# Feed-forward of a decoder layer: the partial sum u4 ahead of the gate's products, p1c ahead of a tap, splits at the entrance shared out differently

## The chip, the cores and the metric

One Trainium2 chip, one of its cores. The metric is the device time of one execution in microseconds (us), lower is better. The engines are TensorE (PE in the profile), VectorE (DVE), ScalarE (ACT), GpSimd (POOL) and SyncE (SP, which here only issues DMA transfers). Each works through its own queue in order; they are tied together by semaphores, and every wait is written out in the kernel.

## The reference

One layer of a decoder on 1024 tokens of width 1024: gated mixing of attention and retention, cross-attention to a memory, and a feed-forward with a causal convolution. The change touches the feed-forward alone:

```python
up = causal_dwconv(rms_norm(h, g_ffn) @ w_up, w_conv, b_conv)   # 1024 -> 5632, three taps along the tokens
a, b = up[..., :D_FF], up[..., D_FF:]                           # D_FF = 2816
h = h + (silu(a) * b) @ w_down
return rms_norm(h, g_final)
```

Everything is float32. The row norm's factor is applied behind the product with `w_up`, and `g_ffn` ahead of it.

## The kernel before

**Splits.** PE multiplies float32 numbers in a rounded form, so each operand is split in two: a rounded high part (ACT copies it: `v_hi` for weights, `parts` for activations) and the rest, the low part (a subtraction: `v_lo` on POOL for weights, `lows` on DVE and a few lines on POOL for activations). Each product of two blocks is three matmuls, high by high, high by low, low by high (`product`, L1265, L1267, L1270).

**Rounds.** The feed-forward's way up runs in 22 rounds, numbered 0 to 21. Round i computes 128 columns of a and the matching 128 of b for all 1024 tokens. It treats these two column blocks and the two halves of the tokens as a 2 x 2 block product and does it in the manner of Strassen and Winograd: seven products instead of eight, each over four blocks of 128 along the inner dimension, so 7 x 4 x 3 = 84 matmuls of 128 x 512 a round. The sums on the activation side (t1 to t4, b2) are made once at the entrance, those on the weight side lie in memory from an earlier stage.

In a steady round PE's order (`seven`) is VA11, VS2, VS1, VS3, VA12, VS4, VA22; rounds 0 and 1 differ a little. The last three add to banks of PSUM that hold an earlier product, and an element-wise engine must have read that first:

- p1c: ACT copies the first product (VA11) from PSUM into the tile u4 (`p1_copy`).
- u2 = p1c + VS2, on DVE (`u_two`, L2721). PE waits for it ahead of VA12.
- u4 = u2 - VS1, on DVE (`u_four`, L2727). PE waits for it ahead of VS4, whose moving operand is b2h.
- c22 = u4 + VS3 (`quarters`, L2777), into zB. PE waits for it ahead of VA22.
- za0, c12 and c21 (L2785, L2789, L2750) bring the other quarters to zA and zB. POOL multiplies three of the four by the norm's factor (`scaled_by`, L624: zb0, zb1, za1).

**Convolution and gate.** A quarter then gets its three taps: ACT the first, with the bias (`tap`, L1942), DVE two more (`conv`, L2117; a1a and a1b for the upper half of a, b0a and b0b for the lower half of b, and so on). ACT applies silu (L1947), and DVE multiplies (`gates_mul`, L2766 and L2768: g0 and g1). ACT issues the store of the gated block yb (`gated_out`, L1952). The convolution and the gate of round i - 1 are done while PE is in round i.

**The order on each queue in a steady round** is written out by hand. DVE: c21, a1a, a1b, b0a, b0b, u2, b1a, b1b, g0, g1, u4, c22, za0, a0a, a0b, c12. ACT: tapA1, tapB1, the copy of VA22's weights, tapB0, silu, p1c, the copies of the next round's VA11, VS2 and VS1, the store of yb (which waits for g1), the copies of VS3 and VA12, tapA0, the copy of VS4, silu. POOL: zb0, the low parts of VA22, and of the next round's VA11, VS2, VS1 and VS3, then zb1, the low parts of VA12 and VS4, za1. The tuples `STEPS`, `TAPS` and `SCALES` name these positions; `v_at`, `a_at` and `p_at` turn a name into the count of the semaphore f_v (DVE), f_a (ACT) or f_p (POOL) at which that step is done. PE waits on these counts. SP loads the next weights as soon as the low part of the slot's last ones is made (`operand_loads`).

**The entrance.** The stage before is a product (`w_xo`) over eight blocks m of 128 channels. While it ends, DVE adds the residual (into hF), ACT squares it for the norm and makes the high part f0h, and DVE makes the low part f0l. From m = 4 on, ACT (`scaled`) and DVE (`mixed`) make the sums t1 to t4 and b2. ACT splits the first weights between blocks: VA11 and VS2 at m = 5, the rest at m = 6. POOL makes the low parts of these, of t3 (L630) and of t4 (L637). Three of the products of round 0 wait for such parts block by block. Between them PE sums the squares with 16 small matmuls, and turns the norm's factors with 8 transposing ones (L1149), which ACT copies to rbF; only then does ACT come to the weights of round 1.

After round 21 comes the way down (`step`), whose first operands are made in the last rounds.

Of the kernel before, what the change touches and what calls it, by code (L numbers as in the profile page):

```python
# [27 lines left out]
H2 = 512  # L28
# [75 lines left out]
STEPS = ("c21", "a1a", "a1b", "b0a", "b0b", "u2", "b1a", "b1b", "g0", "g1", "u4", "c22", "za0", "a0a", "a0b", "c12")  # L104
TAPS = ("tapA1", "tapB1", "tapB0", "silA1", "p1c", "tapA0", "silA0")
# [90 lines left out]
def build(nc, x, mem, pos, slabs, small, const, out):  # L196
# [23 lines left out]
    with ctx:  # L220
# [348 lines left out]
        def _(pool):  # L569
# [63 lines left out]
            pool.wait_ge(S["xT_lo"], lo_at("t1", 3))  # L633
            pool.wait_ge(S["f_p"], CH)
            for k in range(CH):
                pool.wait_ge(S["xT_hi"], hi_at("t4", k))
                pool.tensor_tensor(t4l[:, k, :], hF[:, CH + k, 0:H2], t4h[:, k, :].bitcast(f32), ALU.subtract).then_inc(  # L637
                    S["f_p"], 1)
# [748 lines left out]
        def _(act):  # L1387
# [489 lines left out]
            def p1_copy(i, e):  # L1877

                act.wait_ge(S["p_done"], done_at(i, VA11))
                if not (isinstance(i, int) and i == 0):  # L1880
                    act.wait_ge(S["f_v"], v_at(i - 1, "c22"))
                copy(u4[:, :], ps[:, 4 * e, :]).then_inc(S["f_a"], a_at(0, "p1c") if isinstance(i, int) and i == 0 else 1)
# [25 lines left out]
            for m in range(KB):  # L1908
                for b in range(2):
                    if m == KB - 1 and b == 1:  # L1910
                        act.wait_ge(d_done[1], USE0["xo"] + KB)
                        parts(0, 3)
                    square(1, m, b, USE0["xo"], hF, sq, f0h, "g_ffn")
                act.dma_start(s_y[m], hF[:, m, :]).then_inc(S["h_sp"], 16)
                if m + 2 < KB:
                    act.dma_start(hs[:, m % 2, :], s_h[m + 2]).then_inc(S[f"sa_ld{m % 2}"], 16)
                if m == KB - 1:
                    p1_copy(0, 0)
                if m >= CH:
                    scaled(m - CH)  # L1920
                if m == 5:
                    v_hi(0, VA11)
                    v_hi(0, VS2)
                if m == 6:
                    for v in (VS1, VS3, VA12, VS4):
                        v_hi(0, v)
# [13 lines left out]
            def tap(i, name, c, x_, b, z, y):  # L1940
                apart(act, i)
                act.activation(y[:, half(b)], z[:, 2 + b * H2:2 + (b + 1) * H2], ACT.Identity,  # L1942
                               scale=smc("cw2", c + FB * x_), bias=smc("b_conv", c + FB * x_)).then_inc(
                    S["f_a"], 1)
# [11 lines left out]
            def round_of(i, e, extra=()):  # L1956
# [4 lines left out]
                if not first:  # L1961
# [8 lines left out]
                    if last:  # L1970
                        extra[0]()
                    act.wait_ge(S["f_p"], p_at(i, "zb0"))
                    tap(i, "tapB0", p, 1, 0, zB, yb)
# [4 lines left out]
                    p1_copy(i, e)  # L1978
# [132 lines left out]
        def _(dve):  # L2111
# [612 lines left out]
            def u_four(i, e):  # L2724
# [3 lines left out]
                    S["f_v"], v_at(0, "u4") - v_at(0, "u2") if isinstance(i, int) and i == 0 else 1)  # L2728
# [25 lines left out]
            def gates_of(i):  # L2754
                gates_conv(i)
                gates_mul(i)
# [5 lines left out]
            def gates_mul(i):  # L2762
# [3 lines left out]
                dve.tensor_tensor(yb[:, half(0)], yb[:, half(0)], ya[:, half(0)], ALU.mult).then_inc(S["f_v"], 1)  # L2766
# [75 lines left out]
            dve.wait_ge(S["xT_lo"], lo_at("t1", 3))  # L2842
            dve.memset(zB[:, 0:2], 0.0).then_inc(S["cst"], 1)
            dve.wait_ge(S["cst"], 6)
            quarters(0, 0)
            with dve.Fori(0, (FB - 2) // 2) as i:
                for e in (1, 0):
# [3 lines left out]
                    gates_of(n)  # L2851
                    u_four(n, e)
# [4 lines left out]
            gates_of(n)  # L2857
            u_four(n, 1)
# [8 lines left out]
            gates_mul(FB)  # L2867
# [150 lines left out]
```

## Time and profile before

| | |
|---|---|
| three timed runs | 1844.48, 1847.39, 1847.49 us; median 1847.39 us |
| the profiled execution, its own time | 1844.24 us |
| its span from first to last instruction | 1842.4 us |
| instructions | 25311 |
| PE busy | 1783.6 us (97%) |
| DVE busy | 1076.6 us (58%) |
| ACT busy | 698.7 us (38%) |
| POOL busy | 986.4 us (54%) |
| granted clock of TensorE, mean | 0.99 of full |
| feed-forward, way up | about 1171 to 1616 us of the span |

The profile is one execution. "Busy" of PE counts matmuls that overlap in the pipeline, so 97% doesn't say how closely they follow each other; that is seen in the start times. A row of the order of time gives the start, the duration, the engine, the line of the kernel, the operation and its tiles (output <- inputs), and in brackets how long the engine had been idle ahead of it and which instruction ended that. Lines L1389 (a copy on ACT), L2114 (a low part on DVE) and L2117 (a multiply-add on DVE) are helpers that many steps share, so these are told apart by their tiles. The tiles u2 and u4 both show as u.

### The profile page before, as it was taken

The page shows a single profiled execution, that of the slowest core. Times are in us where ns is not written, and L with a number is a line of the kernel's source. Part 1 is how long each engine was busy: PE and PEld are TensorE (multiplying, and loading weights), DVE is VectorE, ACT ScalarE, POOL GpSimd, SP SyncE. Part 2 cuts the span into 40 slices and gives each one's busy share as a digit, 9 for nine tenths or more (in the row PEclk, how much of TensorE's full clock was granted, in tenths as well). Part 3 has the DMA queues.
Part 4 walks back from the last instruction along what each step waited for, and adds up shares of the span by engine and source line. Part 5 has one row for each costly group of instructions (what it writes and reads, how often), then busy time and mean ns, then how long its engine had stood idle before and what let it go on. Part 6 is the DMA issues. An engine that isn't in the chain of part 4 may idle for free.

```text
span 1842.4 us, 25311 instructions
## 1 busy us (share of the span) xinstructions
PE 1783.6 (97%) x8724; PEld 1481.4 (80%) x8724; DVE 1076.6 (58%) x1549; ACT 698.7 (38%) x1249; POOL 986.4 (54%) x559
## 2 busy tenths in 40 slices
PE   6999999999999899999999989989999999999998
PEld 6788888888887777778878878778888888888887
DVE  5355445101342877885345553877777877789852
ACT  7422223211012666731133222544444444454432
POOL 6833333446664577644532223477777777665540
PEclk9999999999999999999999999899999999999999
DMA  6511111346671688673221224234333333485322
GB/s 261 205 46 35 34 34 46 126 178 210 244 246 45 219 304 322 219 274 128 101 80 47 68 81 138 91 103 135 110 125 126 113 132 119 159 310 175 121 81 92
DMA packets 111054, 261.83 MB, mean 142 GB/s; under 512 B 7680, under 2 KB 50304, under 8 KB 106496
## 3 DMA queue, kind: packets, MB, share of 16 engines
q1 hardware_dynamic: 84720, 182.13, 29.6%
q10 hardware_dynamic: 26256, 78.65, 11.4%
q8 instruction: 50, 0.82, 0.2%
q14 instruction: 28, 0.23, 0.0%
HBM read 186.82 MB, written 73.92 MB: 142 GB/s over the span
## 4 chain that ended last, share of the span: by engine, by line
PE 83%; DVE 7%; ACT 4%; POOL 3%; issue 2%; DMA 1%; SPq 0%; DVEq 0%; ACTq 0%; POOLq 0%
PE ps L690 15%; PE ps L695 15%; PE ps L696 15%; PE ps L1265 7%; PE ps L1270 7%; PE ps L1267 7%; PE ps L1341 3%; PE ps L1340 3%; PE ps L1342 3%; POOL wl L576 1%; ACT prow L1703 1%; PE ps L1069 1%; DVE aneg L2460 1%; DMA raw<-in_slabs 1%; PE ps L1049 1%
## 5 line engine op out<-in xcount | busy, mean ns | idle before, releaser
L583 POOL TENSOR_SCALAR wh<-raw 128x1024 fp32r<-128x1024 f32 x76 | 212.7, 2799 | 496.7 <-PE ps L690 488.0
L690 PE MATMUL ps<-uh,wh 128*128 128x512 f32 (+1 forms) x576 | 228.4, 397 | 2.4 <-POOL wl L585 2.4
L696 PE MATMUL ps<-uh,wl 128*128 128x512 f32 (+1 forms) x576 | 225.2, 391 | 0.0
L695 PE MATMUL ps<-ul,wh 128*128 128x512 f32 (+1 forms) x576 | 224.9, 390 | 0.0
L585 POOL TENSOR_TENSOR wl<-raw,wh 128x1024 fp32r<-128x1024 f32 x76 | 183.5, 2415 | 6.3
L617 POOL TENSOR_TENSOR wl<-raw,wh 128x512 fp32r<-128x512 f32 x88 | 140.9, 1621 | 34.3 <-ACT wh L1389 34.3
L604 POOL TENSOR_TENSOR over_rings<-over_rings 128x512 f32<-128x512 f32 x92 | 118.1, 1285 | 51.7 <-DMA over_rings<-in_slabs 46.1
L2117 DVE SCALAR_TENSOR_TENSOR ya<-zA,sm,ya 128x512 f32<-128x512 f32 x88 | 90.9, 1033 | 81.1 <-ACT ya L1942 73.9
L2117 DVE SCALAR_TENSOR_TENSOR yb<-zB,sm,yb 128x512 f32<-128x512 f32 x88 | 126.6, 1438 | 13.4 <-ACT yb L1942 7.2
L665 POOL TENSOR_TENSOR wl<-raw,wh 128x512 fp32r<-128x512 f32 x63 | 93.9, 1499 | 72.6 <-ACT wh L1389 72.6
L690 PEld LDWEIGHTS ps<-uh,wh 128*128 128x128 f32 (+1 forms) x576 | 107.2, 186 | 25.1 <-POOL wl L585 2.6
L696 PEld LDWEIGHTS ps<-uh,wl 128*128 128x128 f32 (+1 forms) x576 | 107.0, 186 | 25.0 <-issue 0.8
L695 PEld LDWEIGHTS ps<-ul,wh 128*128 128x128 f32 (+1 forms) x576 | 107.2, 186 | 22.9 <-issue 0.5
L1389 ACT ACTIVATE wh<-raw 128x512 fp32r<-128x512 f32 (+1 forms) x163 | 104.1, 653 | 41.4 <-DMA raw<-in_slabs 20.3
L617 POOL TENSOR_TENSOR wl<-ssm,wh 128x512 fp32r<-128x512 f32 x44 | 67.2, 1530 | 74.3 <-ACT wh L1389 74.3
L1342 PE MATMUL ps<-mvh_,wl 128*128 128x512 f32 x252 | 98.0, 389 | 0.0
L1340 PE MATMUL ps<-mvh_,wh 128*128 128x512 f32 x252 | 98.0, 389 | 0.0
L1341 PE MATMUL ps<-mvl_,wh 128*128 128x512 f32 x252 | 98.0, 389 | 0.0
L2356 DVE TENSOR_TENSOR mxr<-ps,sig 128x512 f32<-128x512 f32 x16 | 11.1, 692 | 148.0 <-PE ps L696 148.0
L1265 PE MATMUL ps<-f0h,wh 128*128 128x512 f32 x176 | 69.4, 394 | 5.7 <-DVE u L2721 3.0
L1389 ACT ACTIVATE wh<-ssm 128x512 fp32r<-128x512 f32 x44 | 27.6, 631 | 123.4 <-PE ps L1270 66.2
L1267 PE MATMUL ps<-f0l,wh 128*128 128x512 f32 x176 | 69.1, 393 | 0.0
(461 smaller groups left out, 4914.9 us busy)
## 6 DMA issues: line engine op xcount, KB each, us to landing
raw<-in_slabs SPq DMA_DIRECT2D x110, 512.0 KB, 3.5
over_rings<-in_slabs SPq DMA_DIRECT2D x22, 1024.0 KB, 7.2
s_s<-over_rings SPq DMA_DIRECT2D x22, 1024.0 KB, 4.8
ssm<-s_s SPq DMA_DIRECT2D x22, 512.0 KB, 3.7
raw<-s_s SPq DMA_DIRECT2D x22, 512.0 KB, 4.7
s_f<-yb ACTq DMA_DIRECT2D x22, 512.0 KB, 2.6
raw<-s_d SPq DMA_DIRECT2D x36, 256.0 KB, 2.5
dsum<-in_slabs SPq DMA_DIRECT2D x16, 512.0 KB, 7.1
```

The lines of the kernel that those rows point to most:

```text
L583: pool.tensor_scalar(wh[:, j, :], raw[:, j % RAWS, :], 1.0, None, ALU.mult).then_inc(S["w_hi"], 1)
L585: pool.tensor_tensor(wl[:, j, :], raw[:, j % RAWS, :], wh[:, j, :].bitcast(f32), ALU.subtract).then_inc(S["w_ready"], 1)
L617: pool.tensor_tensor(wl[:, v // 2, half(v % 2)], src, wh[:, v // 2, half(v % 2)].bitcast(f32), ALU.subtract).then_inc(S["v_ready"], 1)
L690: l = pe.matmul(o, lh, rh, start=start, stop=False)
L695: pe.matmul(o, lh, rl, start=False, stop=False)
L696: return pe.matmul(o, ll, rh, start=False, stop=stop)
L1265: l = pe.matmul(ps[:, bank, :], wh_, xh[:, k0 + k, :], start=not more and k == 0, stop=False, skip_group_check=True)
L1267: l = pe.matmul(ps[:, bank, :], wh_, xl[:, k0 + k, :], start=False, stop=False, skip_group_check=True)
L1340: pe.matmul(o, wh[:, j, cm], fh_, start=p == 0 and q < 5, stop=False, skip_group_check=True)
L1341: pe.matmul(o, wh[:, j, cm], fl_, start=False, stop=False, skip_group_check=True)
L1342: l = pe.matmul(o, wl[:, j, cm], fh_, start=False, stop=p == NP - 1, skip_group_check=True)
L2117: return dve.scalar_tensor_tensor(out=o, in0=a, scalar=s_, in1=b_, op0=op0, op1=op1)
```

## The change

1. DVE's order: u4 moves from behind g0 and g1 to between b1b and g0 (`gates_of` now calls `u_four` between `gates_conv` and `gates_mul`). The names in `STEPS` move along, and the counts of the rounds outside the loop are mended to fit.
2. ACT's order: p1c moves from behind tapB0 and the silu to ahead of tapB0, with `TAPS` to match.
3. At the entrance ACT copies VS1 and VS3 of round 0 at m = 5 instead of m = 6.
4. The four low parts of t4 move from POOL to DVE, behind the low parts of b2 and ahead of `quarters(0, 0)`.

```diff
--- before.py
+++ after.py
@@ -101,8 +101,8 @@
 
 VA11, VS2, VS1, VS3, VA12, VS4, VA22 = range(7)
 NV = 7
-STEPS = ("c21", "a1a", "a1b", "b0a", "b0b", "u2", "b1a", "b1b", "g0", "g1", "u4", "c22", "za0", "a0a", "a0b", "c12")
-TAPS = ("tapA1", "tapB1", "tapB0", "silA1", "p1c", "tapA0", "silA0")
+STEPS = ("c21", "a1a", "a1b", "b0a", "b0b", "u2", "b1a", "b1b", "u4", "g0", "g1", "c22", "za0", "a0a", "a0b", "c12")
+TAPS = ("tapA1", "tapB1", "p1c", "tapB0", "silA1", "tapA0", "silA0")
 SCALES = ("zb0", "zb1", "za1")
 
 
@@ -630,12 +630,6 @@
                 pool.tensor_tensor(t3l[:, k, :], hF[:, k, H2:T], t3h[:, k, :].bitcast(f32), ALU.subtract).then_inc(
                     S["f_p"], 1)
             v_lo(0, VA22)
-            pool.wait_ge(S["xT_lo"], lo_at("t1", 3))
-            pool.wait_ge(S["f_p"], CH)
-            for k in range(CH):
-                pool.wait_ge(S["xT_hi"], hi_at("t4", k))
-                pool.tensor_tensor(t4l[:, k, :], hF[:, CH + k, 0:H2], t4h[:, k, :].bitcast(f32), ALU.subtract).then_inc(
-                    S["f_p"], 1)
 
             def round_of(i, extra=None):
 
@@ -1879,7 +1873,7 @@
                 act.wait_ge(S["p_done"], done_at(i, VA11))
                 if not (isinstance(i, int) and i == 0):
                     act.wait_ge(S["f_v"], v_at(i - 1, "c22"))
-                copy(u4[:, :], ps[:, 4 * e, :]).then_inc(S["f_a"], a_at(0, "p1c") if isinstance(i, int) and i == 0 else 1)
+                copy(u4[:, :], ps[:, 4 * e, :]).then_inc(S["f_a"], a_at(0, "tapA0") - 1 if isinstance(i, int) and i == 0 else 1)
 
 
             def scaled(k):
@@ -1919,10 +1913,10 @@
                 if m >= CH:
                     scaled(m - CH)
                 if m == 5:
-                    v_hi(0, VA11)
-                    v_hi(0, VS2)
+                    for v in (VA11, VS2, VS1, VS3):
+                        v_hi(0, v)
                 if m == 6:
-                    for v in (VS1, VS3, VA12, VS4):
+                    for v in (VA12, VS4):
                         v_hi(0, v)
             parts(3, 7)
             acc_hi(1, acc, ach)
@@ -1937,11 +1931,11 @@
             rms_copy(1, rbF)
 
 
-            def tap(i, name, c, x_, b, z, y):
+            def tap(i, name, c, x_, b, z, y, steps=1):
                 apart(act, i)
                 act.activation(y[:, half(b)], z[:, 2 + b * H2:2 + (b + 1) * H2], ACT.Identity,
                                scale=smc("cw2", c + FB * x_), bias=smc("b_conv", c + FB * x_)).then_inc(
-                    S["f_a"], 1)
+                    S["f_a"], steps)
 
             def silu(b):
                 act.activation(ya[:, half(b)], ya[:, half(b)], ACT.Silu).then_inc(S["f_a"], 1)
@@ -1969,13 +1963,14 @@
                         v_hi(i, VA22)
                     if last:
                         extra[0]()
+                    else:
+                        p1_copy(i, e)
                     act.wait_ge(S["f_p"], p_at(i, "zb0"))
-                    tap(i, "tapB0", p, 1, 0, zB, yb)
+                    tap(i, "tapB0", p, 1, 0, zB, yb, 2 if last else 1)
                     act.wait_ge(S["f_v"], v_at(i, "a1b"))
                     silu(1)
                     if last:
                         return
-                    p1_copy(i, e)
                 if extra:
                     extra[0]()
                 else:
@@ -2725,7 +2720,7 @@
                 dve.wait_ge(S["p_done"], done_at(i, VS1))
                 own(i, "u2")
                 dve.tensor_tensor(u4[:, :], u2[:, :], ps[:, 4 * e + 2, :], ALU.subtract).then_inc(
-                    S["f_v"], v_at(0, "u4") - v_at(0, "u2") if isinstance(i, int) and i == 0 else 1)
+                    S["f_v"], v_at(0, "c22") - 1 - v_at(0, "u2") if isinstance(i, int) and i == 0 else 1)
 
             def z_of(z, b):
                 return z[:, 2 + b * H2:2 + (b + 1) * H2]
@@ -2751,19 +2746,20 @@
                 conv(i, p, 0, 1, zA, ya, "tapA1", ("a1a", "a1b"))
                 conv(i, p, 1, 0, zB, yb, "tapB0", ("b0a", "b0b"))
 
-            def gates_of(i):
+            def gates_of(i, e):
                 gates_conv(i)
+                u_four(i, e)
                 gates_mul(i)
 
             def gates_conv(i, steps=1):
                 p = i - 1
                 conv(i, p, 1, 1, zB, yb, "tapB1", ("b1a", "b1b"), steps)
 
-            def gates_mul(i):
+            def gates_mul(i, steps=1):
                 p = i - 1
                 dve.wait_ge(S["f_a"], a_at(p, "silA0"))
                 own(i, "b1b")
-                dve.tensor_tensor(yb[:, half(0)], yb[:, half(0)], ya[:, half(0)], ALU.mult).then_inc(S["f_v"], 1)
+                dve.tensor_tensor(yb[:, half(0)], yb[:, half(0)], ya[:, half(0)], ALU.mult).then_inc(S["f_v"], steps)
                 dve.wait_ge(S["f_a"], a_at(i, "silA1"))
                 dve.tensor_tensor(yb[:, half(1)], yb[:, half(1)], ya[:, half(1)], ALU.mult).then_inc(S["f_v"], 1)
 
@@ -2840,6 +2836,9 @@
             lows(2 * CH, 3 * CH)
             dve.wait_ge(S["f_p"], CH)
             dve.wait_ge(S["xT_lo"], lo_at("t1", 3))
+            for k in range(CH):
+                dve.wait_ge(S["xT_hi"], hi_at("t4", k))
+                lo(t4l[:, k, :], hF[:, CH + k, 0:H2], t4h[:, k, :]).then_inc(S["f_p"], 1)
             dve.memset(zB[:, 0:2], 0.0).then_inc(S["cst"], 1)
             dve.wait_ge(S["cst"], 6)
             quarters(0, 0)
@@ -2848,14 +2847,12 @@
                     n = 2 * i + (2 - e)
                     rest_of(n, e)
                     u_two(n, e)
-                    gates_of(n)
-                    u_four(n, e)
+                    gates_of(n, e)
                     quarters(n, e)
             n = FB - 1
             rest_of(n, 1)
             u_two(n, 1)
-            gates_of(n)
-            u_four(n, 1)
+            gates_of(n, 1)
             move_lo(0)
             quarters(n, 1, (lambda: move_lo(1),))
             move_lo(2)
@@ -2864,7 +2861,7 @@
             move_lo(4)
             gates_conv(FB, 2)
             move_lo(5)
-            gates_mul(FB)
+            gates_mul(FB, 2)
             for n in range(6, NSTEP):
                 move_lo(n)
                 if 0 <= n - 9 < NP:
```

## Rows read from the trace of the kernel before

**Rows 1.** Stretches: length, busy us (x instructions) by engine, PEclk, DMA share, GB/s
```profile
1166.00:1199.00 33.00, 29.26 (x118) 22.77 (x116) 30.95 (x30) 22.41 (x40) 20.77 (x14) 0.84 0.24 80
1262.00:1455.00 193.00, 192.50 (x840) 156.67 (x840) 149.40 (x160) 87.16 (x140) 141.71 (x101) 1.00 0.37 122
```

**Rows 2.** Order of time, PE, rounds 1, 3, 20: start, duration, instruction, [idle]
```profile
1217.04 0.50 PE L1265 MATMUL ps<-f0h,wh 128*128 128x512 f32 x1 [3.00 <-DVE u L2721]
...
1221.75 0.50 PE L1265 MATMUL ps<-b2h,wh 128*128 128x512 f32 x1 [1.69 <-DVE u L2727]
...
1257.53 0.39 PE L1265 MATMUL ps<-f0h,wh 128*128 128x512 f32 x1
...
1260.03 0.39 PE L1270 MATMUL ps<-f0h,wl 128*128 128x512 f32 x1
...
1589.01 0.49 PE L1265 MATMUL ps<-b2h,wh 128*128 128x512 f32 x1
```

**Rows 3.** Order of time, DVE, from round 12 to round 13
```profile
1448.89 2.88 DVE L2117 SCALAR_TENSOR_TENSOR yb<-zB,sm,yb 128x512 f32<-128x512 f32 x2
1451.80 0.69 DVE L2766 TENSOR_TENSOR yb<-yb,ya 128x512 f32<-128x512 f32 x1
1452.41 0.69 DVE L2768 TENSOR_TENSOR yb<-yb,ya 128x512 f32<-128x512 f32 x1
1453.01 0.68 DVE L2727 TENSOR_TENSOR u<-u,ps 128x512 f32<-128x512 f32 x1
...
1464.35 1.30 DVE L2117 SCALAR_TENSOR_TENSOR yb<-zB,sm,yb 128x512 f32<-128x512 f32 x1 [0.41 <-ACT yb L1942]
...
1471.64 0.69 DVE L2768 TENSOR_TENSOR yb<-yb,ya 128x512 f32<-128x512 f32 x1
```

**Rows 4.** Order of time, ACT (ACTq is its queue of DMA issues), same rounds
```profile
1453.30 0.34 ACTq L1952 DMA_DIRECT2D s_f<-yb  x1
1453.77 0.63 ACT L1389 ACTIVATE wh<-ssm 128x512 fp32r<-128x512 f32 x1 [4.82 <-PE ps L1270]
...
1461.40 0.82 ACT L1942 ACTIVATE ya<-zA,sm 128x512 f32<-128x512 f32 x1 [1.66 <-POOL zA L624]
...
1463.35 0.80 ACT L1942 ACTIVATE yb<-zB,sm 128x512 f32<-128x512 f32 x1
...
1464.58 0.58 ACT L1389 ACTIVATE u<-ps 128x512 f32<-128x512 f32 x1
```

**Rows 5.** Order of time, POOL, same rounds
```profile
1454.48 1.30 POOL L617 TENSOR_TENSOR wl<-ssm,wh 128x512 fp32r<-128x512 f32 x1 [3.26 <-ACT wh L1389]
...
1460.20 1.08 POOL L624 TENSOR_TENSOR zA<-zA,rbF 128x512 f32<-128x512 f32 x1
...
1463.52 1.57 POOL L617 TENSOR_TENSOR wl<-a,wh 128x512 fp32r<-128x512 f32 x1 [1.19 <-ACT wh L1389]
```

**Rows 6.** Order of time, POOL, the entrance and round 1
```profile
1170.68 3.43 POOL L617 TENSOR_TENSOR wl<-raw,wh 128x512 fp32r<-128x512 f32 x2
...
1192.47 6.36 POOL L637 TENSOR_TENSOR t4l<-hF,t4h 128x512 fp32r<-128x512 f32 x4
1198.78 3.00 POOL L617 TENSOR_TENSOR wl<-raw,wh 128x512 fp32r<-128x512 f32 x2
...
1208.78 1.09 POOL L624 TENSOR_TENSOR zA<-zA,rbF 128x512 f32<-128x512 f32 x1
```

**Rows 7.** Order of time, DVE, the entrance
```profile
1171.18 1.77 DVE L2117 SCALAR_TENSOR_TENSOR hF<-hF,sm,tx 128x512 f32<-128x512 f32 x1
1172.88 1.78 DVE L2117 SCALAR_TENSOR_TENSOR f0l<-hF,sm,f0h 128x512 fp32r<-128x512 f32 x1
...
1192.55 5.12 DVE L2114 TENSOR_TENSOR b2l<-hF,b2h 128x512 fp32r<-128x512 f32 x3
```

**Rows 8.** Order of time, PE, the entrance
```profile
1177.06 0.50 PE L1265 MATMUL ps<-f0h,wh 128*128 128x512 f32 x1 [2.73 <-ACT u L1389]
...
1195.89 1.03 PE L1149 MATMUL ps<-cn,rsm 128*128 128x128 f32 x8
```

## The prediction

> **What bounds the kernel now.** I read the page first: TensorE is busy nearly everywhere, so a part counts only where PE waits or where something sets PE's pace. The diff touches the feed-forward alone. The stretch table [rows 1] splits it in two: an entrance (1166 to 1199 us) with a granted clock of 0.84, and rounds at clock 1.00 in which PE took 193.00 us for 840 matmuls. A round is 7 products of 12 matmuls, so that is ten rounds of 19.3 us.
>
> PE's order of time [rows 2] says what a round could take: inside a product the starts are (1260.03 - 1257.53) / 11 = 0.227 us apart, 84 x 0.227 = 19.07 us. The first matmul of VS4 (the one on b2h) is at 1221.75 in round 1 and at 1589.01 in round 20: 367.26 / 19 = 19.33 us. So PE loses 0.26 us a round, 4.9 us in 19 rounds, and in PE's order of time the gap lies at that same matmul in each of them, the one that waits for u4. In round 1 it waits 1.69 us for u4 and, a product earlier, 3.00 us for u2 [rows 2].
>
> Why is u4 late by the same small amount every round? I followed it backwards through DVE, ACT and POOL. g1 (L2768) starts at 1452.41 and ends at 1453.10 [rows 3]; ACT issues the store of yb at 1453.30 and then, because its queue is in order, copies wh for VS3 at 1453.77 (the row names PE, but the product it means is long over; it is the store ahead that holds the queue) [rows 4]. POOL had been idle 3.26 us until that copy was done; it starts at 1454.48 and its za1 product ends at 1460.20 + 1.08 = 1461.28 [rows 5]. ACT's tapA1 starts at 1461.40, behind an idle 1.66 us that POOL ended [rows 4]. Then come the two taps on ya, the b0 pair, u2, the b1 pair, g0 and the next g1, at 1471.64 [rows 3]. That is a **closed loop of DVE, ACT and POOL, from g1 to g1**, without PE in it: 19.23 us here and 19.33 in the mean, as PE's own rounds show. PE needs 19.07 and follows the loop. What lengthens g1 to g1 lengthens every round; what only brings u4 forward does not.
>
> **Part 1: u4 ahead of g0 and g1.** u4 is 0.60 us of DVE (1452.41 to 1453.01 is one start to the next) and now lies before g1, in the loop. It gives a little back: g0 reads what b1b wrote and starts only at 1451.80, the pair having ended at 1448.89 + 2.88 = 1451.77, while independent neighbours start 0.09 us before the end of the one ahead (1453.01 against 1453.10) [rows 3]. u4 doesn't read b1b's result and fills that hold of 0.11. g1 comes 0.49 us later, and with it the store, the copy of VS3, POOL's queue (VS3, zb1, VA12, VS4, za1) and tapA1. Nothing absorbs it that I can find: POOL was idle before that copy, not after it. From round 1 to round 20 there are 19 passes: 19 x 0.49 = **+9.3 us**. Bounds: 0.30 a pass (5.7), if a DVE operation that now falls elsewhere beside POOL saves some of it; 0.60 (11.4), without the filled hold. In exchange u4 itself starts 1453.01 - 1451.80 + 0.11 = 1.3 us earlier against its round. That is a gain **once**, -1.3 us, since the loop sets the pace. It is needed in full, as in round 1 PE waited 1.69 us for u4. The last round, 21, is half unrolled with other work in it; PE didn't wait there before, so I count no pass for it.
>
> **Part 2: the copy of the first product (p1c) ahead of tapB0.** ACT's copy lasts 0.58 us (the row at 1464.58) and tapB0 starts that much later than 1463.35 [rows 4]. b0a is next in the loop: it was ready at 1464.35, having waited 0.41 us for tapB0. Yet it took 1.30 us, and ended at 1465.65, 0.56 us after POOL's split of VA22 (1463.52 + 1.57 = 1465.09) [rows 3, 5]. So b0a stood behind POOL's operation. Ready at 1464.93 it would still stand there, and end when it did. Price 0, cover 0.16 us thick. Without the cover it is 0.48 to 0.58 a pass, 19 x 0.5 = 9.5 us; a gain isn't excluded either, since u2 can no longer wait for p1c, but it didn't wait before. The Trainium skill (SBUF — State Buffer, Who interferes with whom) says that a VectorE instruction with two SBUF inputs and a GpSimd instruction that reads SBUF exclude each other for the whole instruction; by that rule the trace agrees (1.30 us for b0a against 0.69 for g1, beside which POOL was idle).
>
> **Part 3: two splits (VS1, VS3) at m = 5 of the entrance instead of m = 6.** ACT and POOL are idle then. POOL did VA12 and VS4 at 1170.68 to 1174.11 [rows 6], behind VS1 and VS3; with those done a block earlier it ends about 3.0 us earlier, at 1171.1. DVE's last f0l at 1172.88 took 1.78 us beside it [rows 7], as did the operation ahead; both (1.77 and 1.78) fall to about 0.7. I take 2.1 off DVE's chain, less 0.25 for what the moved pair costs it at its new place (around 1160, ahead of a wait for PE): 1.85. PE's second product waited 2.73 us (ACT's copy at the end of that chain) [rows 8] and starts 1.85 earlier. Splits and partial sums hang on the same chain, so the entrance shifts by that.
>
> **Part 4: the four t4l from POOL to DVE.** POOL spent 6.36 us on them from 1192.47, and round 1's splits followed at 1198.78 without a pause [rows 6]. These end at the za1 product of 1208.78, which tapA1, b0 and u2 of round 1 stand behind, PE's wait of 3.00. Off POOL, what is late next? ACT's copies for round 1 come behind rbF, and that behind PE's small matmuls at 1195.89 + 1.03 [rows 8], after VS3. These can move only with PE: 1.85 us by part 3, and more if PE keeps its clock (the 0.84 cost it 33 x 0.16 = 5.3 us in the entrance [rows 1], of which I give at most 2.3 to this place). Before, POOL began 1198.78 - 1196.92 = 1.9 us after them; now that is at 1196.9, or down to 1194.6: 1.9 to 4.2 us off round 1. On DVE the four cost 0.6 each beside an idle POOL (g1's 0.60 from start to start [rows 3]), 2.4 us, but b2l ahead of them took 5.12 for three beside POOL [rows 7] and falls to about 1.8. c22 of round 0 then comes near 1196, before VS4 is done: hidden; if DVE stays slow, 4 x 1.7 = 6.8 us, and up to 2 us of it on PE's path. Nothing else changes queue; SP's loads for round 1 stand behind the a22 load and shift with the chain. Parts 3 and 4 together: **-2.4 us**, nearer the slow end, since the waits among which the low clock stood mostly stay. Ends: -4.5 and -1.0.
>
> **Sum.** +9.3 - 1.3 - 2.4 = **+5.6 us**. The profiled execution took 1844.24 us (span 1842.4 and 1.8 around it), so 1849.8; the median of the three timed runs is 3.15 higher. The four executions average 1845.9, and I predict 1851.5. Forecast alone: 5.7 - 1.3 - 4.5 = -0.1 to 11.4 - 1.3 - 1.0 = +9.1, so 1846 to 1855.
>
> **Rivals.**
> A. *PE's gaps are the whole of it* (the other side). u4's wait is the only one PE has in a steady round, and u4 comes 1.3 us earlier: all 4.9 us return, with 1.3 in round 1 and 2.4 at the entrance: -8.6, 1837.3 us. It needs g1 to have room of 0.49 us and the loop to be able to run at 19.07. Against it: POOL's 3.26 us of idleness ended by ACT directly behind the store [rows 5]. The Trainium skill (Perfetto Trace Analysis, Optimization Strategy) tells one to find the gaps of the most-contended engine and make what it waits for start sooner; by that advice the change is right and this rival's time follows. Chance 0.18.
> B. *The later g1 is absorbed but the loop keeps its pace*: rounds of 19.33 as before, and only the gains that come once: -1.3 - 2.4 = -3.7, 1842.2 us. It would need a hidden gap between g1 and tapA1. Chance 0.11.
> C. *The cover of part 2 is too thin*: POOL's split comes earlier or DVE gets the memory first, and tapB0's shift enters the loop: 19 x 0.49 more, 1860.8 us. It decides as soon as b0a is ready after POOL's VA22 split ends. Chance 0.09.
> Forecast 0.62.
>
> **How the numbers follow.** About 0.2% (3.7 us) is what a measurement of this kernel can tell from no change. Slower: five sixths of the forecast, 0.52, and C, 0.09: 0.61. Faster: A and nearly half of B, 0.22. Same: the rest, 0.17. The range goes from 1840, which takes in B and the edge of A, to 1858.
>
> **What the changed profile would show.** g1 start to g1 start 19.8 us; PE's gap ahead of VS4 0.7 to 0.8 us instead of 0.1 to 0.4, and nowhere else in a round; ACT's copy of VS3 0.49 us later after b1b; b0a still ending 0.56 us behind POOL's VA22 split; PE's wait after the first product about 0.9 us; POOL's first split of round 1 near 1197; round 1's VS4 about 3.7 us earlier than 1221.75, round 20's about 5.6 later than 1589.01. I'm wrong if rounds come at 19.1 (A), 19.3 (B) or 20.3 (C).

## The result and the profile after

| | before | after |
|---|---|---|
| timed runs, median (lowest to highest) | 1846.56 (1843.84 to 1847.49) us, 9 runs | 1850.15 (1849.29 to 1853.58) us, 9 runs |
| ratio after to before, 95% interval | | 1.0029 (1.002 to 1.0038) |
| the profiled execution, its own time | 1844.24 us | 1850.15 us |
| its span | 1842.4 us | 1848.3 us |
| DVE, ACT, POOL busy | 1076.6, 698.7, 986.4 us | 1069.2, 693.0, 976.5 us |

The kernel is slower by 0.3%, though three engines are busy for less time and PE's wait at the entrance has shrunk. The medians differ by 3.6 us, the means of the nine runs by 5.05, the spans of the two profiles by 5.9. The time went where the forecast put it, into the rounds; inside, three terms were off and happened to cancel.

The stretches of the changed kernel, in the columns of [rows 1]:

```profile
1166.00:1199.00 33.00, 31.15 (x132) 24.79 (x131) 28.70 (x37) 24.14 (x42) 13.94 (x10) 0.90 0.25 85
1262.00:1455.00 193.00, 189.25 (x821) 152.34 (x820) 142.94 (x158) 81.18 (x136) 139.38 (x98) 1.00 0.35 119
```

The same 193 us of rounds hold fewer instructions on every engine (821 matmuls for 840), while the entrance holds more of PE's (132 for 118) and POOL is busy there for 13.94 us in place of 20.77.

DVE's order of time in rounds 1, 3 and 20 (start, duration, instruction, idle ahead of it):

```profile
1217.67 0.68 DVE L2764 TENSOR_TENSOR yb<-yb,ya 128x512 f32<-128x512 f32 x1
...
1249.96 0.98 DVE L2112 SCALAR_TENSOR_TENSOR yb<-zB,sm,yb 128x512 f32<-128x512 f32 x1 [0.72 <-ACT yb L1936]
...
1253.26 2.88 DVE L2112 SCALAR_TENSOR_TENSOR yb<-zB,sm,yb 128x512 f32<-128x512 f32 x2
1256.06 0.67 DVE L2722 TENSOR_TENSOR u<-u,ps 128x512 f32<-128x512 f32 x1
1256.65 0.68 DVE L2762 TENSOR_TENSOR yb<-yb,ya 128x512 f32<-128x512 f32 x1
1257.26 0.68 DVE L2764 TENSOR_TENSOR yb<-yb,ya 128x512 f32<-128x512 f32 x1
...
1593.35 0.68 DVE L2764 TENSOR_TENSOR yb<-yb,ya 128x512 f32<-128x512 f32 x1
```

g1 starts at 1217.67 in round 1 and at 1593.35 in round 20: 375.68 / 19 = 19.77 us a round, where the kernel before had 19.33. u4 now starts 0.08 us before the b1 pair's end (1253.26 + 2.88 = 1256.14), in place of g0's hold.

What follows g1 on ACT and POOL in round 3, and POOL's split of VA22 half a round earlier:

```profile
1258.14 0.35 ACTq L1946 DMA_DIRECT2D s_f<-yb  x1
1258.62 0.64 ACT L1383 ACTIVATE wh<-ssm 128x512 fp32r<-128x512 f32 x1 [6.76 <-DVE zB L2773]
```

```profile
1248.66 1.75 POOL L617 TENSOR_TENSOR wl<-a,wh 128x512 fp32r<-128x512 f32 x1 [1.31 <-ACT wh L1383]
...
1259.33 1.30 POOL L617 TENSOR_TENSOR wl<-ssm,wh 128x512 fp32r<-128x512 f32 x1 [3.75 <-ACT wh L1383]
```

ACT's copy of VS3 starts 1258.62 - 1256.14 = 2.48 us after the b1 pair, against 1453.77 - 1451.77 = 2.00 before [rows 3, 4]; POOL's idleness ahead of VS3 is 3.75 us for 3.26 [rows 5]. b0a ends at 1250.94, 0.53 us behind POOL's VA22 (1250.41).

PE at the entrance (the second product, the third) and at VS4 in rounds 1, 4 and 20:

```profile
1175.75 0.50 PE L1259 MATMUL ps<-f0h,wh 128*128 128x512 f32 x1 [0.75 <-ACT u L1383]
...
1181.73 0.50 PE L1259 MATMUL ps<-t2h,wh 128*128 128x512 f32 x1 [0.93 <-DVE t2l L2109]
...
1218.29 0.39 PE L1259 MATMUL ps<-b2h,wh 128*128 128x512 f32 x1
...
1275.85 0.39 PE L1264 MATMUL ps<-f0h,wl 128*128 128x512 f32 x1
1276.59 0.49 PE L1259 MATMUL ps<-b2h,wh 128*128 128x512 f32 x1 [0.35 <-DVE u L2722]
...
1592.95 0.49 PE L1259 MATMUL ps<-b2h,wh 128*128 128x512 f32 x1 [0.39 <-DVE u L2722]
```

In round 4 the two starts at VS4 are 0.74 us apart, so 0.51 us are lost (0.45 to 0.56 in rounds 3 to 20), and a further 0.10 us at the next start, which the kernel before loses too. PE's list of waits from 1210 to 1700 us (what it waited for, us in total, times, longest):

```profile
PE ps L1259 <- DVE u L2722: 6.7, 18, 0.4
PE ps L1259 <- DVE u L2716: 2.8, 1, 2.8
PE ps L1334 <- DVE mvl_ L2109: 1.0, 1, 1.0
```

The third line is new, and belongs to the way down. DVE and PE there, first in the kernel before, then in the changed one:

```profile
1625.79 0.68 DVE L2114 TENSOR_TENSOR mvl_<-b,mvh_ 128x512 fp32r<-128x512 f32 x1
```

```profile
1627.24 0.39 PE L1340 MATMUL ps<-mvh_,wh 128*128 128x512 f32 x1
```

```profile
1631.70 0.68 DVE L2109 TENSOR_TENSOR mvl_<-b,mvh_ 128x512 fp32r<-128x512 f32 x1
```

```profile
1632.53 0.47 PE L1334 MATMUL ps<-mvh_,wh 128*128 128x512 f32 x1 [1.00 <-DVE mvl_ L2109]
```

**Where the 5.9 us of span went.** The program up to the feed-forward does not take the same time twice. DVE's first read of that stage's last block from PSUM comes here, before and after:

```profile
1166.28 0.69 DVE L2680 TENSOR_TENSOR hF<-ps,hs 128x512 f32<-128x512 f32 x1 [1.82 <-PE ps L696]
```

```profile
1166.95 0.69 DVE L2675 TENSOR_TENSOR hF<-ps,hs 128x512 f32<-128x512 f32 x1 [1.35 <-PE ps L690]
```

All that follows, the experiments too, is counted from that read ("the mark"), since single spans differ by more than some of the terms. Of the edits only part 3 reaches ahead of it (ACT and POOL do its splits some 8 us earlier), and there too DVE is still waiting for PE at the mark, 1.35 to 1.54 us. Changes against the kernel before:

| place | from the mark, before | after | change |
|---|---|---|---|
| g1 of round 1 | 54.13 | 50.72 | -3.41 (of it +0.49 for standing behind u4: the entrance itself gave -3.9) |
| g1 of round 20 | 421.32 | 426.40 | +5.08 |
| PE's VS4, round 20 | 422.73 | 426.00 | +3.27 |
| end of the span | 676.1 | 681.35 | +5.2 |

19 rounds cost 19 x 0.447 = +8.5. PE comes out of them 3.3 us late, DVE 5.1 us late, and the end of the span is as late as DVE was.

### The profile page after: what moved, and what is told of

Read it like the earlier page. It is cut to its first block, busy times and chain, and to the rows that moved or that the text cites. A ratio compares the mean times of both kernels' runs of the same rounds, so it can differ in the third digit from the quotient of the medians.

```text
span 1848.3 us, 25311 instructions
## 1 busy us (share of the span) xinstructions
PE 1785.5 (97%) x8724; PEld 1480.3 (80%) x8724; DVE 1069.2 (58%) x1553; ACT 693.0 (37%) x1249; POOL 976.5 (53%) x555
## 4 chain that ended last, share of the span: by engine, by line
PE 63%; POOL 13%; issue 12%; DVE 7%; ACT 3%; DMA 1%; POOLq 0%; SPq 0%; DVEq 0%; ACTq 0%
PE ps L684 15%; PE ps L689 15%; PE ps L690 15%; POOL wl L617 10%; PE ps L1334 3%; PE ps L1335 3%; PE ps L1336 3%; POOL zB L624 2%; PE ps L1063 1%; ACT prow L1697 1%; DVE aneg L2455 1%; PE ps L1043 1%; PE ps L1357 1%; PE ps L1359 1%; PE ps L1358 1%
## 5 line engine op out<-in xcount | busy, mean ns | idle before, releaser
L2112 DVE SCALAR_TENSOR_TENSOR ya<-zA,sm,ya 128x512 f32<-128x512 f32 x88 | 100.3, 1140 | 87.5 <-ACT ya L1936 80.4
L2112 DVE SCALAR_TENSOR_TENSOR yb<-zB,sm,yb 128x512 f32<-128x512 f32 x88 | 115.4, 1312 | 23.7 <-ACT yb L1936 17.5
```

Source lines behind the costliest of these rows:

```text
L2112: return dve.scalar_tensor_tensor(out=o, in0=a, scalar=s_, in1=b_, op0=op0, op1=op1)
```

## The experiments

The theory is the closed loop of the prediction, whose pace u4 has lengthened; its first rival is A, which takes PE's waits for the bound. Each kernel is one edit of the kernel before or of the changed one. "A round" is (g1 of round 20 - g1 of round 1) / 19 in its profile.

### Part 1 alone, and the change without it

`u4_only` is the kernel before with part 1; `no_u4` is the changed kernel with part 1 undone.

```diff
-STEPS = (..., "b1a", "b1b", "g0", "g1", "u4", "c22", ...)
+STEPS = (..., "b1a", "b1b", "u4", "g0", "g1", "c22", ...)
                 gates_conv(i)
+                u_four(i, e)
                 gates_mul(i)
...
-                    u_four(n, e)
```

> The kernel before with part 1 alone (u4 ahead of g0 and g1 on DVE). Theory (the closed loop of DVE, ACT and POOL from g1 to g1 sets the rounds, and u4 now lies in it): g1 to g1 goes from 19.33 to 19.77 us as in the changed kernel, 19 passes are +8.5 us at g1 of round 20; PE's VS4 of round 20 is only 7.2 us later, since u4 itself comes 1.3 us earlier in the round, but the way down waits for DVE and takes that back: +8.5 us in all. Rival (PE's waits for u4 are the whole of it; the loss came from p1c delaying tapB0): rounds of 19.07, 1.3 us less wait in round 1, about -6 us in all.

> The changed kernel with part 1 undone: p1c ahead of tapB0 and both edits at the entrance stay. Theory: rounds of 19.33 us as before (the p1c edit costs nothing, because b0a ends 0.55 us behind POOL's split of VA22 either way), the entrance keeps its 3.9 us: round 1's b1b about 3.9 us earlier than before, and so the end: -3.9 us, 7.5 to 8.5 us better than the changed kernel with all its parts. Rival (p1c ahead of tapB0 lengthens the loop): rounds of 19.6 to 19.8 us, +1 to +5 us against before.

Measured: `u4_only` 1853.79 us against 1845.47, ratio 1.0045 (1.003 to 1.0061), a round (1598.54 - 1222.31) / 19 = 19.80 us. `no_u4` 1839.58 us, ratio 0.9967 (0.9954 to 0.9981), a round (1582.49 - 1216.20) / 19 = 19.28. So part 1 costs 0.47 to 0.49 us a round (19.80 against 19.33, 19.77 against 19.28), 9.0 to 9.4 us in 19 rounds, with or without the rest; by the timed runs of `u4_only` it costs 8.3 us, and the other three parts gain 5.9. Rival A falls: with part 1 alone PE's list reads

```profile
PE ps L1265 <- DVE u L2727: 6.1, 17, 0.4
...
PE ps L1340 <- DVE mvl_ L2114: 1.0, 1, 1.0
```

The step that PE waits for was moved forward in its round, and PE waits for it 17 times in the list; in the kernel before the same list names u4 once, with 1.7 us.

**Part 2 gains a little.** It was not tried alone, but parts 3 and 4 leave the rounds at 19.32 and 19.33 us (`splits_only` and `t4l_only` below), so what else separates two kernels is part 2's: 19.28 for 19.33 without part 1, 19.77 for 19.80 with it. The rounds come in pairs, a shorter and a longer one: from g1 to g1 19.22 and 19.44 us in the kernel before, 19.22 and 19.34 in `no_u4`, 19.70 and 19.91 in `u4_only`, 19.72 and 19.83 in the changed kernel. Part 2 takes 0.1 us off the longer one and nothing off the shorter, which is the one that [rows 3] to [rows 5] show. The longer one of the kernel before, whose g1 started at 1471.64, on POOL and DVE:

```profile
1485.20 1.29 POOL L617 TENSOR_TENSOR wl<-raw,wh 128x512 fp32r<-128x512 f32 x1 [0.60 <-ACT wh L1389]
```

```profile
1485.35 1.69 DVE L2117 SCALAR_TENSOR_TENSOR yb<-zB,sm,yb 128x512 f32<-128x512 f32 x1 [0.20 <-DVE yb L2117]
```

and of `no_u4`, on POOL and DVE:

```profile
1480.24 1.30 POOL L617 TENSOR_TENSOR wl<-raw,wh 128x512 fp32r<-128x512 f32 x1 [0.48 <-ACT wh L1383]
```

```profile
1466.79 0.68 DVE L2763 TENSOR_TENSOR yb<-yb,ya 128x512 f32<-128x512 f32 x1
...
1480.50 1.58 DVE L2112 SCALAR_TENSOR_TENSOR yb<-zB,sm,yb 128x512 f32<-128x512 f32 x1 [0.20 <-DVE yb L2112]
```

From g1 POOL's split of VA11 starts after 13.56 us before and after 13.45 with part 2, because ACT's copies ahead of it come 0.11 us earlier. b0b ends 0.54 to 0.55 us behind that split in both, so it, u2 and the next g1 come 0.1 us earlier too.

### The store of yb behind the next two copies

If the loop goes g1, store, copy of VS3, POOL, then ACT's copies of VS3 and VA12 need not stand behind the store that waits for g1. `store_late` does that to the kernel before, `after_store_late` to the changed one.

```diff
-                if not first:
-                    gated_out(i)
                 if extra:
+                    if not first:
+                        gated_out(i)
                     extra[1]()
                 else:
                     v_hi(i + 1, VS3)
                     v_hi(i + 1, VA12)
+                    if not first:
+                        gated_out(i)
```

> The kernel before with one edit: on ACT the store of yb, which waits for g1, is issued behind the copies of VS3 and VA12 instead of ahead of them. Theory: this opens the loop at the place where ACT's in-order queue ties it; POOL's queue then waits for c22 (zb1) instead, about 1.3 us earlier, the loop falls below PE's 19.07 us, PE's waits for u4 vanish from round 3 or so on: rounds of 19.05 to 19.1 us, 19 x 0.26 = -4.9 us. Rival (the tie is not the store's place: DVE's load and its standing behind POOL set 19.33): rounds unchanged, within 1 us of before.

> The changed kernel with the same late store. Theory: rounds of 19.05 to 19.1 us here too, since u4 ahead of g1 costs nothing once g1 is on no loop; with the entrance's 3.9 us and the shorter wait of round 1 the sum is -3.9 - 1.3 - 4.9, near -9 us against before, and PE has no wait for u4 at all. If the order u4, g0, g1 costs by itself (c22 comes no earlier than before, and zb1 hangs on it), the gain over before is only some 4 us and rounds stay at 19.3 or more.

Measured: `store_late` 1866.69 us against 1845.47, ratio 1.0112 (1.0095 to 1.0128), a round (1608.94 - 1223.79) / 19 = 20.27: the opposite of what I expected. `after_store_late` 1836.91 us, ratio 0.9953 (0.9938 to 0.9967), a round (1580.88 - 1217.76) / 19 = 19.11: as expected, PE's own pace with hardly a wait. Of the first, PE's list says

```profile
PE ps L1265 <- DVE u L2729: 19.6, 20, 1.1
```

and in the orders of time of DVE, PE and POOL, one round of it:

```profile
1466.68 1.78 DVE L2770 TENSOR_TENSOR yb<-yb,ya 128x512 f32<-128x512 f32 x1
1468.38 0.67 DVE L2729 TENSOR_TENSOR u<-u,ps 128x512 f32<-128x512 f32 x1
...
1472.95 1.83 DVE L2119 SCALAR_TENSOR_TENSOR ya<-zA,sm,ya 128x512 f32<-128x512 f32 x1 [0.20 <-DVE ya L2119]
1474.70 0.67 DVE L2791 TENSOR_TENSOR zA<-u,ps 128x512 f32<-128x512 f32 x1
```

```profile
1469.18 0.49 PE L1265 MATMUL ps<-b2h,wh 128*128 128x512 f32 x1 [1.12 <-DVE u L2729]
```

```profile
1466.09 1.82 POOL L617 TENSOR_TENSOR wl<-ssm,wh 128x512 fp32r<-128x512 f32 x1 [0.60 <-ACT wh L1389]
...
1472.94 1.29 POOL L617 TENSOR_TENSOR wl<-raw,wh 128x512 fp32r<-128x512 f32 x1 [0.73 <-ACT wh L1389]
1475.45 1.09 POOL L624 TENSOR_TENSOR zA<-zA,rbF 128x512 f32<-128x512 f32 x1 [1.22 <-DVE zA L2791]
```

Brought forward, POOL's split of VS3 (1466.09 to 1467.91) falls onto g1, which takes 1.78 us instead of 0.68, and ends 0.55 us behind it. u4 stands behind g1, so it is 1.1 us later; PE waits 1.12 us for it and starts VS4 late; ACT's copy of the VS4 weights waits 0.80 us for PE; POOL's split of VS4 waits for ACT and now falls onto a0b (1.83 us; in the kernel before a0b took 1.50). c12 and with it POOL's za1, **idle for 1.22 us where the kernel before had none ahead of it**, come late, and so does tapA1. There is a second closed path, from u4 over c22, za0, tapA0, a0a, a0b and c12 to za1, with a branch from u4 through PE's VS4. My prediction had seen only the first.

In the changed kernel the same edit finds u4 ahead of g1. POOL's VS3 split then lengthens only g0, which u4 doesn't wait for; in `after_store_late`:

```profile
1465.09 1.18 DVE L2764 TENSOR_TENSOR yb<-yb,ya 128x512 f32<-128x512 f32 x1
```

### An extra operation of the same length, ahead of g1 or behind it

To weigh the two paths by themselves, DVE reads the bank of PSUM once more (0.68 us, 0.60 from start to start, the result is not used), in the changed order ahead of u4 and so of g1 (`extra_ahead`), or in the old order behind g1 and ahead of u4 (`extra_behind`).

```diff
                 own(i, "u2")
+                if not (isinstance(i, int) and i == 0):
+                    dve.tensor_reduce(amax[:, 0, 0:1], ps[:, 4 * e + 2, :], AX.X, ALU.max)
                 dve.tensor_tensor(u4[:, :], u2[:, :], ps[:, 4 * e + 2, :], ALU.subtract)
```

> The kernel before with part 1, and in each round from 1 on one more VectorE operation that nothing needs, a reduction of the same PSUM bank (128 x 512, about 0.6 us), ahead of u4 and so ahead of g0 and g1. Theory: it lies in the loop from g1 to g1 in full: rounds of 19.80 + 0.6 = 20.4 us, and 19 x 0.6 = 11 us more than part 1 alone, about +20 us against before. Rival (VectorE has room in a round, 19.3 of which it is busy for some 15): rounds as with part 1 alone, 19.8 us.

> The kernel before, with the same extra operation ahead of u4, but g0 and g1 stay ahead of both: it lies behind g1. Theory: g1 and the store aren't touched, so the loop keeps 19.33 us; u4 is 0.6 us later in the round, once. But u4 also leads through PE's VS4, ACT's copy of the next VS4 and POOL's split to za1, a path that was about 0.6 us shorter than the one by g1, so it may just begin to show: rounds of 19.3 to 19.5 us, 0 to +4 us. Rival (any work on VectorE before PE's operand costs its own length every round): 19.9 us, +12 us.

Measured, one execution each: `extra_ahead` 1869.74 us, a round (1609.16 - 1221.60) / 19 = 20.40, so +0.60 on the 19.80 of `u4_only`, as expected. In all it is 23.7 us above the kernel before, some 4 more than expected, and from the mark 3.9 of its 25.3 us come on the way down, where PE waits 2.1 us for a low part of POOL. `extra_behind` 1860.04 us, a round (1602.77 - 1220.17) / 19 = 20.14, so +0.81 on 19.33, where I expected up to 0.2 and the rival said 0.6. An operation behind g1 costs more than its own length. DVE's order of time in it, and POOL's:

```profile
1461.89 0.69 DVE L2770 TENSOR_TENSOR yb<-yb,ya 128x512 f32<-128x512 f32 x1
1462.49 0.68 DVE L2728 TENSOR_REDUCE amax<-ps 128x1 f32<-128x512 f32 x1
...
1466.34 1.76 DVE L2117 SCALAR_TENSOR_TENSOR ya<-zA,sm,ya 128x512 f32<-128x512 f32 x1 [1.24 <-ACT ya L1942]
...
1469.72 0.68 DVE L2791 TENSOR_TENSOR zA<-u,ps 128x512 f32<-128x512 f32 x1
```

```profile
1465.20 1.10 POOL L624 TENSOR_TENSOR zB<-zB,rbF 128x512 f32<-128x512 f32 x1
1466.25 3.00 POOL L617 TENSOR_TENSOR wl<-raw,wh 128x512 fp32r<-128x512 f32 x2
...
1470.48 1.09 POOL L624 TENSOR_TENSOR zA<-zA,rbF 128x512 f32<-128x512 f32 x1 [1.23 <-DVE zA L2791]
```

and the same place in the kernel before, on DVE and on POOL:

```profile
1456.26 1.12 DVE L2117 SCALAR_TENSOR_TENSOR ya<-zA,sm,ya 128x512 f32<-128x512 f32 x1 [1.24 <-ACT ya L1942]
...
1459.00 0.68 DVE L2789 TENSOR_TENSOR zA<-u,ps 128x512 f32<-128x512 f32 x1
```

```profile
1455.73 1.10 POOL L624 TENSOR_TENSOR zB<-zB,rbF 128x512 f32<-128x512 f32 x1
1456.78 3.45 POOL L617 TENSOR_TENSOR wl<-raw,wh 128x512 fp32r<-128x512 f32 x2
```

In each case a0a becomes ready while POOL is at work, and ends 0.55 us behind the operation that it finds there. Before, that is zb1, which ends at 1456.83: a0a ends at 1457.38, and it is POOL's split of VA12 (the first of the pair), begun in the meantime, that takes longer, 1.75 us. In `extra_behind` a0a is ready 0.09 us after that split has begun: the split takes 1.30 us and ends at 1467.55, and a0a takes 1.76 and ends at 1468.10. The 0.60 us of the extra operation have become 1.24 us at a0a's end. From g1 to za1 it is 1470.48 - 1461.89 = 8.59 us, against 1460.20 - 1452.41 = 7.79 before: +0.80, the whole +0.81. The rest of the 1.24 went into the room that the old order had there: za1 came 0.52 us after c12's end (1460.20 against 1459.68), and now comes 0.08 after it.

### The entrance: each part alone

`splits_only` is the kernel before with part 3, `t4l_only` with part 4.

```diff
                 if m == 5:
-                    v_hi(0, VA11)
-                    v_hi(0, VS2)
+                    for v in (VA11, VS2, VS1, VS3):
+                        v_hi(0, v)
```

```diff
-            for k in range(CH):
-                pool.wait_ge(S["xT_hi"], hi_at("t4", k))
-                pool.tensor_tensor(t4l[:, k, :], ...)
...
+            for k in range(CH):
+                dve.wait_ge(S["xT_hi"], hi_at("t4", k))
+                lo(t4l[:, k, :], hF[:, CH + k, 0:H2], t4h[:, k, :]).then_inc(S["f_p"], 1)
```

> The kernel before with part 3 alone (VS1 and VS3 split at m = 5). Theory: DVE's chain of the entrance comes 2.0 us earlier (POOL is out of its way at the last f0l), PE's wait behind the first product falls from 2.7 to 0.7 us; t4l stays on POOL and ends 2.0 us earlier, so round 1 and the end come 2.0 us earlier. Rounds 19.33. Rival (the entrance's gain is t4l's alone): 0.

> The kernel before with part 4 alone (the four low parts of t4 on DVE). Theory: POOL is free early, but ACT's copies for round 1 stand behind PE's small matmuls, which nothing moves: POOL starts round 1's splits at 1198.7 instead of 1198.8; with less in DVE's way round 1 comes 0.1 to 1 us earlier. The part pays only together with part 3, whose 2.0 us become 3.9 with it. Rival (POOL's 6.4 us were the bound by themselves): -2 us or more.

Measured: `splits_only` 1844.34 us against 1846.0, ratio 0.9993 (0.9984 to 1.0002); `t4l_only` 1843.91, ratio 0.9991 (0.9982 to 1.0). Both intervals reach 1, so the profiles decide, from the mark to g1 of round 1: `splits_only` 52.07, that is -2.06; `t4l_only` 53.37, -0.76; both together -3.8 (`no_u4`, 50.31). They give more together than the sum of 2.8, and POOL shows why. First `splits_only`, then `t4l_only`, then the changed kernel:

```profile
1194.91 6.82 POOL L637 TENSOR_TENSOR t4l<-hF,t4h 128x512 fp32r<-128x512 f32 x4
1201.70 2.53 POOL L617 TENSOR_TENSOR wl<-raw,wh 128x512 fp32r<-128x512 f32 x2
```

```profile
1200.61 2.55 POOL L617 TENSOR_TENSOR wl<-raw,wh 128x512 fp32r<-128x512 f32 x2 [6.07 <-ACT wh L1383]
```

```profile
1196.19 2.59 POOL L617 TENSOR_TENSOR wl<-raw,wh 128x512 fp32r<-128x512 f32 x2 [4.96 <-ACT wh L1383]
```

From the mark, round 1's first split starts at 32.50 before, 31.01 with part 3 alone (POOL is still at t4l), 32.29 with part 4 alone (POOL idles, waiting for ACT's copy behind rbF, behind PE), 29.24 with both. Each part takes away one of two bounds that lay close together.

### The first partial sum and the late store together, and the fastest version

`u4_store_late` is the kernel before with part 1 and the late store: two edits that cost 8.3 and 21.2 us by themselves. `all_za1_early` is the changed kernel with the late store, and in round 0 alone POOL's za1 stands directly behind zb1:

```diff
                 scaled_by(i, "zb1", zB, 1, v_at(i, "c22"), 2 if first else 1)
+                if first:
+                    scaled_by(i, "za1", zA, 1, v_at(i, "c12"))
                 for v in (VA12, VS4):
...
-                scaled_by(i, "za1", zA, 1, v_at(i, "c12"))
+                if not first:
+                    scaled_by(i, "za1", zA, 1, v_at(i, "c12"))
```

> The kernel before with two edits: u4 ahead of g0 and g1 (alone +8.3 us) and the store of yb behind the copies of VS3 and VA12 (alone +21 us). Theory: a round has two closed paths, one by g1, the store and POOL's queue, one by u4, c22, PE's VS4 and c12 to za1. Each edit alone shortens the one and lengthens the other; together g1 is on neither and u4 is 1.1 us (g0 and g1) earlier on the second. So rounds of 19.1 us, PE's own pace; round 1 waits 1.3 us less for u4: -1.3 - 19 x 0.23 = -5.7 us against before. Rival (the costs of the two edits add): +29 us.

> The changed kernel with the late store and, in round 0 alone, POOL's za1 product directly behind zb1, ahead of the splits of VA12 and VS4. With the late store PE waits only at the entrance, 2.74 us of it in round 1 for u2, which stands behind tapA1 and tapB0. Theory: za1 comes about 2.4 us earlier, but zb0 of round 1, which tapB0 needs, stays behind the two splits: u2 and the end 1.2 us earlier than with the late store alone, -9.8 us against before, ratio 0.9947. Rival (za1 wasn't what round 1 waited for): -8.6 us.

Measured, against 1845.35 us for the kernel before (14 runs; a fifteenth took 6317.33 us and is not counted): `u4_store_late` 1840.79 us, 4.6 less, ratio 0.9979 (0.9964 to 0.9993), a round (1581.06 - 1216.95) / 19 = 19.16; from the mark its span ends 3.2 us earlier. Both gains are below the 5.7 us expected: u4's wait of 1.7 us in round 1 is gone, but the one for u2 ahead of it is 4.1 us for 3.0. `all_za1_early` 1835.16 us, ratio 0.9949 (0.993 to 0.9968), a round (1580.02 - 1216.95) / 19 = 19.11; PE's wait for u2 in round 1 is 2.0 us for the 2.7 of `after_store_late`. It has the lowest median made here, 10.2 us below the kernel before. But the intervals of the two overlap, and from the mark their spans end within 0.2 us of each other, so that za1's new place gains anything is not shown.

That the two harmful edits gain together follows from the two paths. Part 1 shortens the path from u4 and lengthens the one from g1. The late store cuts the path from g1, but POOL's split now falls on the product that DVE does at that time: g1 in the old order, with u4 behind it, and g0 in the new one, which u4 doesn't wait for. The late store in turn makes g1's lateness harmless.

## Why the prediction was right, and which of its steps were not

The forecast of +5.6 us met +5.9 of span (+5.2 from the mark), and its 1851.5 us a median of 1850.15. Point by point:

- **Part 1, the closed loop and its pace: right.** Its 0.49 us a round measured 0.47 (`u4_only` against the kernel before) and 0.49 (the changed kernel against `no_u4`), so 9.0 to 9.4 us for the 9.3 written. Rounds of 19.8 were forecast, 19.77 measured. The gap ahead of VS4 is 0.5 us, smaller than the 0.7 to 0.8 written, since PE loses its 0.65 us a round (19.72 less 19.07) in two places, 0.55 there and 0.10 at the start behind it. The kernel before lost 0.06 and 0.27 us there by turns, and the same 0.10.
- **Part 2 at nothing: wrong by a little.** The cover held: b0a, ready later, ends 0.53 us behind POOL's VA22, as the forecast's 0.56 had it. What the forecast missed is that p1c, once ahead of the silu, brings ACT's next copies forward by 0.11 us in every second round. It had read a round of the other kind. From g1 of round 1 to g1 of round 20 that is 366.29 us for 367.19 without part 1 and 375.68 for 376.23 with it: a gain of 0.6 to 0.9 us. This, and not a smaller cost of part 1, is why the rounds together cost 8.5 us and not 9.3. Part 2 was not tried alone.
- **Parts 3 and 4: mechanism right, size wrong.** The term of -2.4 us measured -3.9 (-3.8 without part 1). The two operations of DVE that fell from 1.8 to 0.7 us are f0l, as written, and the one on tx at the head of that chain; the one directly ahead of f0l still takes 1.77. Part 3 alone gave 2.06 for the 1.85 written; it is part 4's share, 0.55 in the sum, that came to 0.76 alone and to 1.8 in company. PE's wait after the first product fell from 2.73 to 0.75 (0.9 forecast), and a new one of 0.93 us for t2l took part of it back, which I hadn't foreseen. The clock in the same stretch was 0.90 for 0.84, and POOL's first split of round 1 started 3.3 us earlier from the mark, in the middle of the 1.9 to 4.2 for which I had taken the slow end; from there to za1 POOL's queue was a further 0.5 us shorter.
- **The one-off gain of -1.3: wrong, it was not kept.** It is there at PE's VS4 of round 20: from the mark +3.27, which is 8.5 - 3.9 - 1.3. (In round 1 VS4 came 4.1 us earlier from the mark, for 3.7 forecast and the 3.9 + 1.3 that the terms allow. After its wait for u2 PE went through VA12 at a granted clock of 0.62, from 1213.84 to 1218.30 us, so VS4 started 1.1 us behind u4's end at 1217.15.) It is gone again on the way down. The step that failed is "The last round, 21, is half unrolled ...; PE didn't wait there before, so I count no pass for it." DVE is 5.1 us late behind the rounds; the low part that step 5 waits for (`mvl_`, 1631.70) had 0.8 us of room before (its end 1626.47, PE's first matmul of step 5 at 1627.24), and now PE waits 1.00 us for it. That and two smaller pauses of PE, 4 us ahead of it and 36 us behind, bring PE up to DVE's lateness. The sum that fits is +8.5 - 3.9 + 0.6 = +5.2, where the last term is DVE's path in place of PE's: g1's own +0.49, and 0.1 gathered behind it. That the end meets DVE's lateness so closely is in part luck: with nothing changed in that stretch `no_u4` and `t4l_only` lost a further 1.0 and 0.9 us there, at other waits, and what makes the second small pause is not known.
- **So the errors cancelled, and that is luck.** The forecast had 1.5 us too little gain at the entrance and 0.8 us too much cost in the rounds, 2.3 us to the slow side together, and 1.9 us to the fast side at the end, where -1.3 should have been +0.6. The total was closer than its parts.
- **What the prediction said of the loop was incomplete.** It read as if only the path through ACT's store bounded the rounds, and from that I expected `store_late` to gain; it cost 21.2 us. For `extra_behind` I knew of a second path from u4 and gave it 0.6 us of room; it had 0.44 (the 0.52 less the 0.08 that stay), and the order at POOL added 0.64. Part 1 was priced rightly because it shortens the second path and lengthens the first.
- **Rival A** (PE's gaps are the whole) fell with `u4_only`: rounds of 19.80 for the 19.07 that it needs. The advice in the Trainium skill (Perfetto Trace Analysis, Optimization Strategy), to make what the most contended engine waits for start sooner, misled here until the loop was cut too; with the store moved as well (`after_store_late`) it holds: rounds of 19.11, and 1836.9 us. **Rival B** (19.33 kept) and **rival C** (20.3) fell with the 19.77 of the changed kernel.

Left open: part 1 costs 8.3 us by the medians of `u4_only` and the kernel before. The changed kernel and `no_u4` were not timed side by side; each against its own runs of the kernel before gives 3.6 + 5.9 = 9.5. The intervals overlap and no run separates them further. Nor was it tried whether the new wait for t2l at the entrance can be taken away.

## What to carry to other kernels

An in-order queue ties its neighbours into closed paths, so the wait that the busiest engine shows may be the pace of a loop it has no part in: measure the round from one start to the next, compare it with what that engine needs, and before moving a step write down every path back to the same instruction with its slack, not only the one that decides now. Two edits that each lose can gain together, and two that each gain little can gain more, where two bounds lie within a microsecond of each other; try them together before dropping them. A stretch behind a loop can inherit the lateness of the engine that set the pace, and not that of the one that was measured. And where rounds come in pairs, a single round read from the trace can miss what a change does to the other kind.

## What the runs showed of the hardware

- **DVE's operations with two SBUF inputs and POOL's take turns, and what DVE finds POOL at decides a round.** A DVE operation that became ready while POOL was at work ended 0.53 to 0.56 us behind POOL's operation: b0a before and after, b0b in the longer rounds, g1 in `store_late` (1.78 us for 0.68), a0a behind zb1 in the kernel before and behind the split in `extra_behind`. POOL's split of VA12 took 1.75 us when it began while a0a was under way, and 1.30 when it began first. The Trainium skill (SBUF — State Buffer, Who interferes with whom) states the exclusion, and the traces agree with it; that a shift of 0.6 us in the order turns into 0.8 us a round is `extra_behind`'s.
- **Code that no one changed moves by several microseconds from one execution to the next.** In the seven profiles of kernels without part 3, which are the same up to the mark, it lay between 1161.90 and 1168.77 us; in all twelve between 1161.90 and 1170.69. Terms of 1 or 2 us can be read only from a mark inside the same execution, or from many timed runs.
